# Two layer-block networks on one core: where the squares of the modulated norms are summed, and what lies around their spread

## The reference

```python
def rmsnorm(x, g):
    y = xf * lax.rsqrt(jnp.mean(xf * xf, axis=-1, keepdims=True) + NORM_EPS)
    return y.astype(x.dtype) * g

def modulate(x, g, shift, scale):
    return rmsnorm(x, g) * (1 + scale) + shift
```

## Time and profile before

| | us |
|---|---|
| median of 3 runs | 3092.02 (3090.35 to 3096.43) |
| profiled execution | 3096.14 |
| its span, first to last instruction | 3094.1 |
| TensorE busy | 2927.1 (95%) |
| VectorE busy | 1623.5 (52%) |
| ScalarE busy | 1287.0 (42%) |
| GpSimd busy | 168.2 (5%) |
| mean granted TensorE clock | 0.974 |

### The profile page before, as it was taken

The page is one execution under the profiler, slowest core; times in us unless marked ns, Lnnn a source line. Parts: engine busy times, 40 slices in busy tenths (PEclk is TensorE's granted clock), DMA queues, the critical chain, the costliest instruction groups (busy, mean ns, idle before and its releaser), DMA issues.

```text
span 3094.1 us, 51584 instructions
## 1 busy us (share of the span) xinstructions
PE 2927.1 (95%) x17930; PEld 2504.7 (81%) x17930; DVE 1623.5 (52%) x3043; ACT 1287.0 (42%) x2511; POOL 168.2 (5%) x120
## 2 busy tenths in 40 slices
PE   7999999999999999899998878999999999989998
PEld 7979789799797897688885546788878888768998
DVE  5566775555667655432335786423334333438554
ACT  4445455455454454422333443422333223325454
POOL 0000010000010100000001770000000000000000
PEclk9999999999999999999999989999999999989999
DMA  7556265565562656433334761423323333242553
GB/s 247 186 166 212 83 195 184 165 194 180 181 211 79 194 184 184 155 107 95 102 89 143 254 229 55 136 85 110 104 80 112 98 101 101 76 142 67 160 182 99
DMA packets 239198, 443.14 MB, mean 143 GB/s; under 512 B 26416, under 2 KB 27440, under 8 KB 238384
## 3 DMA queue, kind: packets, MB, share of 16 engines
q1 hardware_dynamic: 237632, 433.47, 44.2%
q0 software_dynamic: 1392, 7.34, 0.7%
HBM read 439.65 MB, written 1.05 MB: 142 GB/s over the span
## 4 chain that ended last, share of the span: by engine, by line
PE 82%; DVE 11%; POOL 3%; issue 2%; ACT 1%; DMA 1%; SPq 0%; DVEq 0%; ACTq 0%; POOLq 0%
PE ps L753 81%; DVE low L1807 2%; POOL hidden L2431 2%; DMA raw<-weights 1%; DVE ps L1810 1%; DVE hidden L1810 1%; DVE zl L1810 1%; DVE hidden L1807 1%; DVE x L1813 1%; POOL low L2401 1%; DVE zl L1807 1%; DVE coef L2354 1%; DVE hidden L2358 1%; DVE neg_max L2153 1%; DVE hidden L2180 0%
## 5 line engine op out<-in xcount | busy, mean ns | idle before, releaser
L753 PE MATMUL ps<-zh,low 128*128 128x256 f32 (+1 forms) x4192 | 1397.8, 333 | 87.8 <-DVE low L1807 41.5
L753 PE MATMUL ps<-zl,high 128*128 128x256 f32 (+1 forms) x4192 | 1383.4, 330 | 0.0
L753 PE MATMUL ps<-zh,high 128*128 128x256 f32 (+1 forms) x4192 | 1382.5, 330 | 0.0
L1807 DVE TENSOR_TENSOR low<-raw,high 128x512 fp32r<-128x512 f32 x1276 | 844.2, 698 | 430.4 <-ACT high L1343 428.5
L1343 ACT ACTIVATE high<-raw 128x512 fp32r<-128x512 f32 x1304 | 764.8, 625 | 605.6 <-PE ps L753 511.0
L753 PEld LDWEIGHTS ps<-zh,low 128*128 128x128 f32 x4192 | 807.2, 193 | 197.1 <-issue 55.1
L753 PEld LDWEIGHTS ps<-zh,high 128*128 128x128 f32 x4192 | 807.6, 193 | 69.6
L753 PEld LDWEIGHTS ps<-zl,high 128*128 128x128 f32 x4192 | 808.3, 193 | 66.6
L1807 DVE TENSOR_TENSOR hidden<-gated,ps 128x256 f32 (+1 forms) x176 | 91.5, 520 | 604.1 <-ACT gated L1343 604.1
L1343 ACT ACTIVATE gated<-ps 128x256 f32<-128x256 f32 (+1 forms) x176 | 81.3, 462 | 494.2 <-PE ps L753 494.0
L753 PE MATMUL ps<-high,zl 128*128 128x512 f32 (+2 forms) x544 | 196.7, 362 | 3.8 <-DVE zl L1807 3.8
(11 more groups left out here) (201 smaller groups left out, 1933.4 us busy)
## 6 DMA issues: line engine op xcount, KB each, us to landing
raw<-weights SPq DMA_DIRECT2D x1642, 256.0 KB, 3.3
hidden<-norms POOLq DMA_DIRECT2D x4, 1024.0 KB, 6.5
cst<-consts SPq DMA_DIRECT2D x1, 1830.0 KB, 12.9
x<-x_in SPq DMA_DIRECT2D x1, 1024.0 KB, 6.0
x<-tokens_in POOLq DMA_DIRECT2D x1, 1024.0 KB, 12.4
x<-ctx_in POOLq DMA_DIRECT2D x1, 1024.0 KB, 6.1
out<-hidden POOLq DMA_DIRECT2D x1, 1024.0 KB, 5.1
```

The source lines that it names most:

```text
L753: return nc.tensor.matmul(out, lhsT, rhs, start=first, stop=last, **kw)
L1807: return nc.vector.tensor_tensor(out, a, b, op)
```

## The change

GpSimd adds the squares of tiles 1 to 5 onto that of tile 0, in norms 2 to 7 (`sum_squares`); TensorE then makes power groups for three tiles, the sum, 6 and 7 (`summed_power`), and `follow` is gone. Norm 1 keeps eight groups. TensorE now puts six of the fill's eight quarters ahead of the spread and two behind it, and turns the row before behind the fill (norm 1: ahead of its groups; norm 2: between the sum's group and group 6; norm 6: ahead of all groups). In norm 1, and where there is no fill, four fillers stand ahead of the spread instead of two; behind it there is one filler instead of four (norm 2 keeps four, norm 6 twelve). ScalarE copies the fill's row between its second and third piece (the "n == 1" line). A row copy that was pending is taken ahead of the squares. VectorE's early columns are taken ahead of the reciprocal, and the splitting is spread differently over the pieces.

```diff
--- before.py
+++ after.py
@@ -46,6 +46,7 @@
 LATE_FILLS = 3
+SUMMED = 6
 PAD = (TAPS - 1) // 2
@@ -486,6 +487,7 @@
         sq_ready = sem("sq_ready")
+        power_summed = sem("power_summed")
         std_ready = sem("std_ready")
@@ -856,7 +858,6 @@
                             m.then_inc(y_ready, 1)
-                        self.follow(T, d)
@@ -916,10 +917,15 @@
-            def follow(self, T, d):
-                if d >= 2:
-                    self.power_of(T, d - 2)
+            def summed_power(self, T, early=False):
+                self.seen(sq_ready, SUMMED)
+                self.pe.wait_ge(power_summed, self.seen(power_summed, SUMMED - 1))
+                self.power(T, 0, 0)
+                if early:
+                    self.turn_rows(2)
+                for k in range(SUMMED, KT):
+                    self.power_of(T, k)
@@ -938,15 +944,15 @@
-            def fill_rows(self, rows):
+            def fill_rows(self, rows, ks=range(KT)):
...
                     self.pe.wait_ge(cs_ready, 1)
-                for k in range(KT):
+                for k in ks:
                     w = self.raw_quarter()
...
                     self.done(self.mm(ps[strip, rows, :], cs[:, k, :], w, k < 4, k >= 4))
-                self.fills += 1
+                self.fills += KT - 1 in ks
@@ -983,18 +989,27 @@
             def pre_norm(self, T, n, l):
-                for k in range(KT) if (n, l) == (0, 0) else (6, 7):
-                    self.power_of(T, k)
-                if has_fill(n, l):
+                early = has_fill(n, l) and self.turns < fills_before(l, n)
+                if not has_fill(n, l) and self.turns < fills_before(l, n):
+                    self.turn_rows(3)
+                if (n, l) == (0, 0):
                     self.turn_rows(7)
-                elif self.turns < fills_before(l, n):
-                    self.turn_rows(3)
-                assert self.turns >= fills_before(l, n)
-                self.stream(2, 1)
+                    for k in range(KT):
+                        self.power_of(T, k)
+                else:
+                    self.summed_power(T, early)
+                begun = 6 if has_fill(n, l) and (n, l) != (0, 0) else 0
+                if begun:
+                    self.fill_rows(6, range(0, begun))
+                else:
+                    self.stream(4, 1)
                 self.spread(T, 4)
                 if has_fill(n, l):
-                    self.fill_rows(6)
-                self.stream(4 if has_fill(n, l) else 12, 1)
+                    self.fill_rows(6, range(begun, KT))
+                    if not early and (n, l) != (0, 0):
+                        self.turn_rows(7)
+                assert self.turns >= fills_before(l, n)
+                self.stream((4 if early else 1) if has_fill(n, l) else 12, 1)
@@ -1261,7 +1275,6 @@
                     self.tile(y_tile(512, d), 512)
-                    self.follow(512, d)
@@ -1320,8 +1333,7 @@
             def finish(self):
-                for k in (6, 7):
-                    self.power_of(S, k)
+                self.summed_power(S)
                 self.spread(S, 4)
@@ -1451,6 +1463,8 @@
                     self.f(r(zh[:, k, cols]), self.src[:, k, cols], func, bias=bias(k, h)).then_inc(norm_ready, 1)
+                    if n == 1:
+                        self.take_rows()
                     if n in splits:
@@ -1498,11 +1513,9 @@
                 self.ahead(-5)
-                self.take_rows()
-                self.ahead(-4)
                 act.wait_ge(mods_ready, 9 * l + 3 * n + 1)
                 self.src = wide
-                self.scaled(T, ACT.Identity, lambda k, h: mods[:, 3 * n, k, h:h + 1], (1, 4, 7, 10) if T == 512 else (0, 2, 4, 6))
+                self.scaled(T, ACT.Identity, lambda k, h: mods[:, 3 * n, k, h:h + 1], (3, 5, 7, 10) if T == 512 else (0, 2, 4, 6))
                 self.ahead()
@@ -1974,11 +1987,11 @@
                     self.filled()
+                if early:
+                    self.take_cols(2 if has_fill(n, l) else 3)
+                assert self.taken >= fills_before(l, n)
                 self.recip_of(T)
-                if early:
-                    self.take_cols(7 if has_fill(n, l) else 3)
-                assert self.taken >= fills_before(l, n)
-                self.ahead(-7 if T == 512 else -5)
+                self.ahead(-6 if T == 512 else -5)
                 v.wait_ge(mods_ready, 9 * l + 3 * n + 2)
@@ -1997,7 +2010,7 @@
                         if k == 0 and h == per - 1:
-                            self.ahead(-4)
+                            self.ahead(-5 if T == 512 else -4)
                         if k in (1, 3, 5, 7) and h == per - 1:
@@ -2400,6 +2413,13 @@
+            def sum_squares(T, before, norms_before):
+                for k in range(1, SUMMED):
+                    pool.wait_ge(sq_ready, before + k + 1)
+                    if k > 1:
+                        pool.wait_ge(power_summed, norms_before * (SUMMED - 1) + k - 1)
+                    nc.gpsimd.tensor_tensor(square[:, 0, 0:T], square[:, 0, 0:T], square[:, k, 0:T], ALU.add).then_inc(power_summed, 1)
             for m in range(2 * DEPTH):
@@ -2412,6 +2432,8 @@
             pool.dma_start(x[:, :, S:512], ctx_in).then_inc(ctx_landed, 16)
+            sum_squares(512, KT, 0)
@@ -2434,6 +2456,9 @@
                     low_of(n + 2, 1)
+            squares = 2 * KT + KT // 2
+            for m, T in enumerate((512, 512, 512, S, S)):
+                sum_squares(T, squares + KT * m, m + 1)
             pool.wait_ge(result_ready, 1)
```

## The result

The changed kernel took 3058.1 us (median of 4 runs, 3054.92 to 3060.22) against 3094.22 for the kernel before (4 runs, 3090.35 to 3098.8): a ratio of 0.9876, 95% interval 0.9862 to 0.9891. The forecast was 3057. The profiled execution took 3056.17 us, of which 3054.4 is span; the mean granted clock was 0.979 (0.974 before). Matmuls now carry line 755, VectorE's lines 1820 (lows), 1823 (residuals, hidden, zl) and 1981 (reciprocal), ScalarE's 1355, GpSimd's sum 2421.

What follows compares the result with a forecast made beforehand. TensorE held 82% of the chain; the cost lay in power groups inside production and VectorE's row behind the spread. 11.8 + 2.15 + 2.56 - 0.5 + 0.35 + 14.7 + 3.8 = 34.9 us off 3092.0 gives 3057, range 3046 to 3072.

Steps and rivals of the forecast that it cites:

- Powers out of the production: Norms 2 to 7: power groups leave tile production, gaining 2.95 us each in norms 2 to 5, 2.15 and 2.56 after.
- The recorded sign: What would show it: residuals of norms 2 to 5 all 1.36 us apart, about 8.1 us from second to eighth.
- GpSimd's sum: Norms 2 to 7: five adds take 7.05 us at 512 columns, done 0.9 us before the eighth square, cost 0.
- five are 3.5 us against 4.3, cost 0: Norm 7: 128x256 adds taken at half of 1.41 us, so the sum costs nothing; at full 1.41, 2.9 us lost.
- Contention: VectorE beside GpSimd's adds: residuals keep 0.88 us; norm 6's low splits could each lose up to one add, cost 0.
- the cover that was named: Norm 6: VectorE idles 3.33 us per pair, so lows slowed by GpSimd's adds cost 0.
- Behind the spread: Norms 2 to 5: VectorE's row starts earlier, seventh quarter at 16.5 us instead of 20.5 in norm 4; 14.7 us gained.
- Norm 1: Fill stays behind the spread, fourth quarter holds the first product; gain 3.8 us, between 1.5 and 4.9.
- Norm 2: Row turn between groups 0 and 6 costs 0.5 us (0 to 1.1); earlier row behind the spread gains 2.4.
- Norms 5 to 7: Root to root: 6.25 us gained from norm 5 to 6, 2.9 from norm 6 to 7.
- The fourth rival: Narrow matmuls drop the clock to 1.2 GHz in the five 512-column norms, 10 us each: 3107; chance 0.04.
- The second rival: Shorter TensorE gaps keep the clock up in norms 1, 2, 5 and 6, some 7 us more: 3050; chance 0.07.

Runs made afterwards that it cites:

- shorter sum: The changed kernel with GpSimd's sum in the 256-column norms 6 and 7 over five tiles, TensorE summing four: 3053.2 us, ratio 0.9865.
- row copy first: The changed kernel with the row copy back ahead of the first zh, the fill still split around the spread: 3063.41 us, ratio 0.9899.
- fill behind: The changed kernel with all eight quarters of the fill behind the spread, four fillers ahead of it: 3060.37 us, ratio 0.9893.
- before, both fillers: The kernel before with throwaway products added in the convolution and in attention's first group, nothing else: 3092.17 us, ratio 0.9988.
- changed, again: The changed kernel itself, unaltered, measured once more against the kernel before: 3056.45 us, ratio 0.9867.
- order alone: The changed kernel with eight power groups back inside the production and no sum on GpSimd: 3073.76 us, ratio 0.9931.
- sum alone: The kernel before with only GpSimd's sum and three power groups; fill, turn, row copy and splits unmoved: 3081.41 us, ratio 0.9952.
- GpSimd sums eight: The changed kernel with all eight squares summed by GpSimd and one power group on TensorE: 3073.5 us, ratio 0.9931.
- both fillers, shorter sum: The changed kernel with throwaway products in the convolution and attention, and one GpSimd add fewer in norms 6 and 7: 3048.22 us, ratio 0.9849.

## Why the prediction was right, step by step

**Powers out of the production: right, in norm 3 a little less.** The residuals stand 1.36 us apart in norms 2, 4 and 5. The recorded sign named norm 3 too, which was wrong: with 24 matmuls a tile its residuals stand 5.44 apart (6.03 before), and only four of the five intervals became shorter, 2.4 us for 2.95. Norm 3 to 4 gained 7.0 (forecast 7.15), norm 4 to 5 6.8 (6.95). In norm 7 the pairs stand 1.44 us apart, 12 products at 0.12.

**GpSimd's sum: right for 512 columns, 0.4 us short for 256.** Five adds take 7.03 us in norms 2, 4 and 5 (7.05 from the earlier trace rows) and end 1.05 us before the eighth square does (forecast 0.9). In norm 7 (GpSimd, then TensorE):

```profile
3037.36 0.73 POOL L2421 TENSOR_TENSOR hidden<-hidden 128x256 f32<-128x256 f32 x1 [196.40 <-ACT hidden L1355]
3038.41 3.36 POOL L2421 TENSOR_TENSOR hidden<-hidden 128x256 f32<-128x256 f32 x4 [0.32 <-ACT hidden L1355]
```
```profile
3041.83 0.54 PE L755 MATMUL ps<-hidden,cst 128*32 128x64 f32 x24 [1.59 <-POOL hidden L2421]
```

An add takes 0.73 us, near the half that was taken, but a chain of them goes at 0.84, and the second waits for its square. The sum ends at 3041.77, 0.16 us behind the eighth square, and three groups stand behind it instead of one. The step "five are 3.5 us against 4.3, cost 0" failed; the price is 0.4, as the shorter sum shows.

**Contention: as forecast, with its size.** The residuals beside the adds keep their 0.88 us. VectorE's lows, with both inputs in SBUF, do not, in norm 6 (VectorE, then GpSimd):

```profile
2832.74 3.61 DVE L1820 TENSOR_TENSOR low<-raw,high 128x512 fp32r<-128x512 f32 x4
```
```profile
2832.96 1.06 POOL L2421 TENSOR_TENSOR hidden<-hidden 128x256 f32<-128x256 f32 x1 [3.49 <-ACT hidden L1355]
2834.46 0.74 POOL L2421 TENSOR_TENSOR hidden<-hidden 128x256 f32<-128x256 f32 x1 [0.44 <-ACT hidden L1355]
```

Four lows took 2.50 us before and take 3.61 beside two adds. By this the rule of the Trainium skill (SBUF — State Buffer, "Who interferes with whom") holds for both forms. It costs nothing, since the next pair waits for TensorE in any case, 5.76 us behind the last; that is the cover that was named.

**Behind the spread: right.** In norms 3, 4 and 5 the first zl starts 1.26 us behind the spread's end (forecast 1.26), and the seventh quarter's wait stands at 16.53 us in norms 3 and 4 (16.5). A small term was wrong: six quarters of the fill were taken as six eighths of 1.92 us, 1.44, and take 1.89. A fill is eight matmuls, one a quarter, each recorded twice. `fill_rows` gives quarters 0 to 3, and then 4 to 7, one of the array's four 32-column strips each. In the trace the records of different strips start 7 ns apart, in sets that follow each other by 0.43 us: four full sets for the eight quarters before, two full and two half ones for the six now, which take as long. The spread ends 0.1 us later for it.

**Norm 1: under-sized.** From its root to the last zl 23.6 us before, 18.4 after: 5.2 gained, where 3.8 was taken and 4.9 was the bound. The fourth quarter did not hold anything: TensorE's first wait behind its first product is 0.39 us. The bound was passed by the 0.3 us by which the spread now ends sooner (2.53 us behind the root, 2.84 before); the clock, 0.77 over the 22 us before and 1.00 after, fits that.

**Norm 2: mis-sized, and not settled.** The turn between groups 0 and 6 cost the 0.5 us that was taken: the root starts 1.70 us behind the start of the eighth square, 1.17 before. Up to the convolution's second half-group 1.9 us were gained (2.4 forecast), but at the convolution's own root the changed kernel stood 0.7 us behind: 2.6 taken back. The clock at half in the second half-group explains 1.2 of it in this trace. From the first zl on the convolution took 223.4 us here, 224.0 in the second trace of the same kernel, and 219.9 to 220.9 in three variants that differ little in it (row copy first, fill behind, shorter sum). What makes it scatter, and whether the change has a part in it, stays open.

**Norms 5 to 7: under-sized by the clock.** The order's 4.0 us behind norm 5's spread are there (4.1 forecast), and norm 6's production is 2.2 us shorter (2.15): of its three intervals between pairs two lose 0.87 us and one 0.43. The remaining 3.4 of the 9.6 us lie in the attention. Behind its first projections the granted clock was 0.50 from 75 to 99 us behind norm 5's root before the change, and from 70 to 80 in the changed kernel (windows at the same distance from the root, before and after):

```profile
2762.00:2782.00 20.00, 18.43 (x80) 10.20 (x79) 5.63 (x16) 6.21 (x15) 0.00 (x0) 0.50 0.66 211
```
```profile
2736.00:2756.00 20.00, 17.76 (x117) 10.74 (x110) 10.61 (x31) 8.29 (x22) 0.00 (x0) 0.99 0.59 211
```

That part is no steady gain of the change. In the kernel with the shorter sum alone, which has the same order, the clock was 0.50 from 72 to 96 us, and the stretch took 192.6 us, 5.7 less than before where 6.25 was forecast; the second trace of the changed kernel took 190.2.

Norm 6's first product comes 2.0 us earlier behind the root (4.78 instead of 6.76), 0.35 of it forecast; the rest is again the clock, 0.92 before and 1.00 after over 22 us. The kernel before with both fillers, at 1.00 and in the old order, bears this out: 5.17, of which the order is worth 0.4.

**How far the close number is luck.** The forecast of 34.9 us met 36.1. The terms of the two mechanisms came out where a stretch holds nothing else, but that the total came so close rests also on errors that cancel, in this pair of traces 2.0 us too little in norm 1 to 2, 3.7 too much in the convolution, 3.4 and 1.3 too little in the last two stretches, and these move from trace to trace with the clock.

**The clock, seen over all.** The granted clock over the 22 us from each root, norms 1 to 6, one trace each:

| kernel | 1 | 2 | 3 | 4 | 5 | 6 |
|---|---|---|---|---|---|---|
| before | .77 | .98 | 1.00 | 1.00 | .74 | .92 |
| before, both fillers | .77 | .84 | .84 | 1.00 | 1.00 | 1.00 |
| changed | 1.00 | .89 | 1.00 | 1.00 | .69 | 1.00 |
| changed, again | 1.00 | .94 | 1.00 | 1.00 | .84 | 1.00 |
| order alone | 1.00 | 1.00 | 1.00 | 1.00 | .77 | 1.00 |
| sum alone | .84 | .84 | .77 | .84 | .61 | .92 |
| GpSimd sums eight | .92 | .77 | .95 | .94 | .81 | .84 |
| both fillers, shorter sum | .96 | 1.00 | 1.00 | 1.00 | 1.00 | 1.00 |

The fourth rival (the clock falls everywhere) did not come true for the change. The clock did fall in every norm in the traces of the sum without the order and of the sum of eight; for the latter, in norm 4, it came right behind a wait of 3.40 us. For the sum alone the cause is open: norms 2 and 3 of "before, both fillers" run the code of the kernel before, and have 0.84 where that kernel has 0.98 and 1.00. The second rival (the clock stays up, 3050) came half true, in norms 1 and 6; with fillers where TensorE waits the clock is 0.96 to 1.00 in all six norms, at a median of 3048.

## What to carry to other kernels

Take reduction work out of a production only as far as the helper engine ends before the last input does: at 6 of 8 tiles of 512 columns GpSimd's sum ended 1.05 us early and cost nothing, in the last norm it ended 0.16 us late and cost 0.4, at 8 of 8 it cost 17 us, some 7 of them with the slower clock behind the wait. When an engine stands at a copy for another engine's by-product, move the copy behind the pieces that others wait for: 1.8 us a norm here. Where TensorE must wait some 3 us between two full groups, throwaway products in the wait are worth a look, and a stage that scatters by 4 us between traces is no place to read a 2 us effect from one. Compare traces from a common point behind the part that nobody changed: here that part alone moved by 12 us.

## What the runs showed of the hardware

- GpSimd's float32 add of two SBUF tiles: 128x512 in 7.03 us for five in a chain (1.41 each), 128x256 in 0.73 alone and 0.84 in a chain; beside VectorE's lows, which read two SBUF tiles, 1.06 for the first of two and 0.74 for the second.
- VectorE's 128x512 subtraction of two SBUF tiles: four in 2.50 us alone, in 3.61 beside GpSimd's adds; its form with one tile in PSUM keeps its time.
- The granted clock fell to 0.50 (1.2 GHz) behind waits of TensorE of 3.3 to 3.4 us, but around one and the same wait of 3.30 us it fell just ahead of the group in one trace, 1.2 us into it in another, and in two others not at all. With twelve products of 512 columns in that wait, some 3 us in all, the group ran at the full clock in all four kernels that had them.
- Records of float32 matmuls of 512 columns in different 32-column strips of the array start 7 ns apart, and sets of them 0.43 us apart: six quarters of a fill took 1.89 us, eight 1.92.
